# Retention stage of a fused two-block layer: values centred per token, output products with tokens on partitions, row norm per token block, and a new order of the first gate product

## What is computed

```python
u = rms_norm_2(h, ret_norm_pre[i])
q, k, v, g = jnp.split(u @ ret_w_in[i], ...)
q = rope(...); k = rope(...) * (RET_QK_DIM ** -0.5)
o = retention_chunkwise(q, k, v)          # per head: (scores * decay) @ v
mu = jnp.mean(o, axis=-1, keepdims=True)  # over the 512 value columns of a head
var = jnp.mean(jnp.square(o - mu), axis=-1, keepdims=True)
o = (o - mu) * lax.rsqrt(var + EPS)
o = merge_heads(o) * jax.nn.silu(g)
y = o @ ret_w_out[i]                      # 2048 -> 1024
h = h + rms_norm_2(y, ret_norm_post[i])   # norm over the 1024 columns of a token
kv = rms_norm_2(h, kv_norm) @ w_kv        # read by the stick-breaking layer
```

## Time and profile before

| what | value |
|---|---|
| median of 3 runs | 1977.68 us |
| the three runs | 1977.68, 1975.15, 4728.48 us |
| the profiled execution, own time | 1978.11 us |
| its span in the trace | 1976.3 us |
| granted TensorE clock over the span | 0.995 |
| PE busy | 98% |
| DVE busy | 59% |
| ACT busy | 36% |
| HBM read | 169.50 MB |

### The profile page before, as it was taken

How to read it: one execution, slowest core, us unless ns; L and a number is a source line. 1 busy time by engine, 2 the same in 40 slices (tenths; PEclk the granted TensorE clock), 3 DMA queues, 4 the chain that set the end, 5 groups by cost and what they waited for, 6 DMA issues and landing times.

```text
span 1976.3 us, 24001 instructions
## 1 busy us (share of the span) xinstructions
PE 1932.6 (98%) x9302; PEld 1615.8 (82%) x9302; DVE 1172.1 (59%) x1379; ACT 711.1 (36%) x759; POOL 14.2 (1%) x23
## 2 busy tenths in 40 slices
PE   7999999999999999999999999999998999999998
PEld 5888888788878888888888788888886788888886
DVE  5334355677655574434355749494949765556656
ACT  4323233336352233322233223232323644444445
POOL 0000000000000000000000000000000000000000
PEclk9999999999999999999999999999999999999999
DMA  4222223321112222232223322221212112221222
GB/s 169 96 102 89 93 76 101 133 70 63 61 38 99 104 86 107 85 106 85 86 88 102 138 86 86 75 94 65 104 65 85 54 65 86 86 85 68 80 85 65
DMA packets 27448, 173.44 MB, mean 88 GB/s; under 512 B 3200, under 2 KB 3232, under 8 KB 10368
## 3 DMA queue, kind: packets, MB, share of 16 engines
q1 hardware_dynamic: 24912, 165.95, 23.8%
q0 software_dynamic: 1328, 4.61, 0.8%
q10 hardware_dynamic: 1152, 2.10, 0.3%
HBM read 169.50 MB, written 3.15 MB: 87 GB/s over the span
## 4 chain that ended last, share of the span: by engine, by line
PE 91%; DVE 5%; ACT 3%; issue 1%; DMA 0%; DVEq 0%; ACTq 0%
PE acc L1524 27%; PE acc L1525 27%; PE acc L1526 27%; PE att L1525 2%; PE att L1526 2%; PE att L1524 2%; ACT tmp L542 1%; PE att L1935 1%; PE att L1934 1%; ACT tmp L534 1%; DVE w_lo L837 0%; PE att L1964 0%; DMA h<-in_x 0%; PE att L1562 0%; PE att L1980 0%
## 5 line engine op out<-in xcount | busy, mean ns | idle before, releaser
L1524 PE MATMUL acc<-x_hi,w_hi 128*128 128x512 f32 x1400 | 551.4, 394 | 14.8 <-DVE w_lo L837 14.7
L1526 PE MATMUL acc<-x_hi,w_lo 128*128 128x512 f32 x1400 | 546.4, 390 | 0.0
L1525 PE MATMUL acc<-x_lo,w_hi 128*128 128x512 f32 x1400 | 546.3, 390 | 0.0
L837 DVE TENSOR_TENSOR w_lo<-raw,w_hi 128x2048 fp32r<-128x2048 f32 (+1 forms) x166 | 378.5, 2280 | 127.5 <-ACT w_hi L411 123.7
L411 ACT ACTIVATE w_hi<-raw 128x2048 fp32r<-128x2048 f32 (+1 forms) x166 | 315.2, 1899 | 105.7 <-PE acc L1526 101.8
L1524 PEld LDWEIGHTS acc<-x_hi,w_hi 128*128 128x128 f32 x1400 | 263.6, 188 | 72.7 <-DVE w_lo L837 16.1
L1525 PEld LDWEIGHTS acc<-x_lo,w_hi 128*128 128x128 f32 x1400 | 263.5, 188 | 56.3 <-issue 2.4
L1526 PEld LDWEIGHTS acc<-x_hi,w_lo 128*128 128x128 f32 x1400 | 263.4, 188 | 55.5
L1524 PE MATMUL acc<-g_hi,w_hi 128*128 128x512 f32 x352 | 137.2, 390 | 0.0
L1526 PE MATMUL acc<-g_hi,w_lo 128*128 128x512 f32 x352 | 137.1, 389 | 0.0
L1525 PE MATMUL acc<-g_lo,w_hi 128*128 128x512 f32 x352 | 137.1, 389 | 0.0
(11 more groups left out here) (315 smaller groups left out, 2871.9 us busy)
## 6 DMA issues: line engine op xcount, KB each, us to landing
raw<-in_ffn_up SPq DMA_DIRECT2D x44, 1024.0 KB, 4.7
raw<-in_ret_head SPq DMA_DIRECT2D x24, 1024.0 KB, 4.7
raw<-in_ffn_down SPq DMA_DIRECT2D x32, 704.0 KB, 4.0
raw<-in_mix_gate SPq DMA_DIRECT2D x8, 1024.0 KB, 4.7
raw<-in_ret_out SPq DMA_DIRECT2D x8, 1024.0 KB, 4.7
raw<-in_sb_v SPq DMA_DIRECT2D x8, 1024.0 KB, 4.7
raw<-in_sb_kq SPq DMA_DIRECT2D x8, 1024.0 KB, 4.7
raw<-in_sb_g SPq DMA_DIRECT2D x8, 1024.0 KB, 4.7
```

The source lines that it names most:

```text
L837: tt(w_lo[:, slot, 0:cols], raw[:, slot, 0:cols], w_hi[:, slot, 0:cols].bitcast(F32), ALU.subtract).then_inc(w_ready, 1)
L1524: mm(dst, still[0], move[0], start=first, stop=False)
L1525: mm(dst, still[0], move[1], start=False, stop=False)
L1526: return mm(dst, still[1], move[0], start=False, stop=last)
```

## The change

Six things are changed; the arithmetic of the rest stays.

1. Values. ACT reads each bank of values twice: a copy with scale -1/512 whose accumulator gives minus the mean of the token (`neg_mean`), and a second one that adds it as a bias. DVE's low part uses the same number. As the mean over value columns is linear, the head's outputs then have mean zero. The scale of the token (`r_tok`), which the values carried, goes to the scores.
2. The mean of the outputs (L1856), the copies out of `att`, the three additions and the four subtractions go. ACT squares the outputs in `att`, DVE multiplies them there with the gate and frees the bank, and three additions give the sum of squares.
3. The output product takes tokens on partitions: the gated outputs are the stationary side, the weights (laid out anew) the moving one. It has as many passes as before. The norm of the head becomes one number per token (`norm_columns`: four float32 products of 128 columns, issued before the fourth bank), and one DVE instruction per bank scales and adds.
4. In the last head both gate pairs come before `rs` x `rv`, and the output product starts with each gated chunk as it comes.
5. The norm over a token's 1024 columns is taken on ACT by the accumulator of a square, for each block of 128 tokens; ACT scales the first half of the block, DVE the second, and 32 transposes of 128 x 128 float32 on PE (`turn_y`, `turn_y_late`) bring the result back to features on partitions, 16 ahead of the first `kv` chunk and 16 among the chunks. DVE then makes `h` in one instruction from `att`. Of the 36 unread products 6 and 8 are left. The slab of the keys is made in quarters.
6. The first gate product of the mixture comes before the attention branch's products, the second behind them.

```diff
@@ ScalarE, values
+                    nc.scalar.activation(rv_hi[:, k, :], bank, ACT.Copy, scale=-1.0 / TOK,
+                                         accum_out=neg_mean[:, k:k + 1]).then_inc(act_step, 1)
+                    act.wait_ge(act_step, step.next())
+                    nc.scalar.activation(rv_hi[:, k, :], bank, ACT.Identity, bias=neg_mean[:, k:k + 1]).then_inc(hi_ready, 1)
...
@@ ScalarE, last head, second half of the columns
+                    for m in range(TB):
+                        if m == TB - 1:
+                            prep_part(0)
+                        square_rows(1, m)
...
+                        nc.scalar.activation(row_std[:, m:m + 1], half_sq[:, 1, m:m + 1], ACT.Sqrt, scale=1.0 / D,
+                                             bias=half_mean[:, m:m + 1]).then_inc(fn_ready, 1)
+                        act.wait_ge(row_scaled, m + 1)
+                        nc.scalar.activation(y_ret[:, 2 * m, :], y_ret[:, 2 * m, :], ACT.Copy,
+                                             scale=row_scale[:, m:m + 1]).then_inc(z_first, 1)
...
@@ VectorE
+            def gated(c):
+
+                dve.wait_ge(fn_ready, fn.next())
+                dve.wait_ge(sq_ready, squared.next())
+                tt(r_gate[:, c, :], att[:, b.k % BANKS, :], r_gate[:, c, :], ALU.mult).then_inc(att_free, 1)
+                b.next()
...
+                    for m in range(TB):
+                        outputs(1, m, m + 1)
+                        if m == TB - 1:
+                            prep_part(0, keys_part_ready)
+                        scale_rows(m)
+                        if m == 1:
+                            prep()
...
@@ TensorE
-                pair()
-                pe.wait_ge(op_ready, op.next())
-                mm(side_bank(), mean_v[:], t(4), start=True, stop=True).then_inc(att_full, 1)
-                pair()
...
+                def norm_columns():
+
+                    pe.wait_ge(ssq_ready, sq.at())
+                    dst = side_bank()
+                    b.next(RET_SKIP)
+                    for m in range(TB):
+                        ins = mm(dst[:, m:m + P], ssq[:, plain[m]], mean_v[:], start=True, stop=True)
+                    ins.then_inc(att_full, 1 + RET_SKIP)
...
+                    if last and m >= 2:
+                        if m == 2:
+                            turned_y.extend((side_bank(), side_bank(), side_bank(), side_bank()))
+                        turn_y(turned_y, m - 2)
...
+                turn_y(turned_y, TB - 2)
                 keys, query, vals = bank(), bank(), [bank(), bank()]
...
+                spare(6)
+                turn_y(turned_y, TB - 1)
+                spare(8)
...
                 for c in range(DC):
+                    if 1 <= c <= DC - TB:
+                        turn_y_late(c + TB - 1)
...
+                        gate = slab()
+                        project(gate, DC, x)
+                        pe.wait_ge(att_free, b.at(BANKS))
+                        for k in range(2):
+                            project(branch[0], 6 * k, (o_hi, o_lo), 2)
+                        project(gate, 0, x)
```

More of the change, by code:

```diff
@@ L661, in gate, with square_head, split_gated, square_rows @@
                     s.next()
-            def outputs(first, end, last):
-                for c in range(first, end):
-                    val.next()
-                    if last:
-                        act.wait_ge(val_ready, val.at())
-                        square(c, y_ret[:, c, :])
+            def square_head(c):
+                act.wait_ge(att_full, b.next())
+                nc.scalar.activation(r_sq[:, c, :], att[:, (b.k - 1) % BANKS, :], ACT.Square).then_inc(sq_ready, 1)
+            def split_gated(c, first, dst):
+                act.wait_ge(att_free, b.at(first - b.k + c + 1 + BANKS))
+                nc.scalar.activation(dst[:, c, :], r_gate[:, c, :], ACT.Copy).then_inc(hi_ready, 1)
+            def square_rows(half, m):
+                act.wait_ge(acc_free, u.at(m + 1) + BANKS)
+                nc.scalar.activation(t(m), y_ret[:, 2 * m + half, :], ACT.Square,
+                                     accum_out=half_sq[:, half, m:m + 1]).then_inc(act_step, 1)
+                step.next()
             def ret_body(last):
@@ L679, in ret_body @@
                 gate(r_gate[:, 0:2, :])
[L680 to L683 removed]
+                if last:
+                    gate(r_gate[:, 2:4, :])
+                first = b.k
+                if last:
+                    for c in range(RET_VC + 1):
+                        if c < RET_VC:
+                            square_head(c)
+                        if c:
+                            split_gated(c - 1, first, by_chunk(rqk_hi))
+                else:
+                    for c in range(RET_VC):
+                        square_head(c)
+                    gate(r_gate[:, 2:4, :])
                     prep()
                     s.next(2)
[L686 to L688 removed]
+                    for c in range(RET_VC):
+                        split_gated(c, first, rv_hi)
                     prep()
@@ L1829, in ret_values, with turn_y, turn_y_late @@
                         ins.then_inc(seg_done, 1)
+            def turn_y(banks, m):
+                pe.wait_ge(z_first, m + 1)
+                for c in range(TB):
+                    ins = nc.tensor.transpose(banks[c][:, plain[m]], y_ret[:, 2 * m, plain[c]], ident[:])
+                    if m == TB - 1:
+                        ins.then_inc(att_full, 1)
+            def turn_y_late(c):
+                pe.wait_ge(h_ready, 2 * DC + c - TB + 1)
+                dst = att[:, b.k % BANKS, :]
+                b.next()
+                for m in range(TB):
+                    if c == TB:
+                        pe.wait_ge(z_second, m + 1)
+                    ins = nc.tensor.transpose(dst[:, plain[m]], y_ret[:, 2 * m + 1, plain[c - TB]], ident[:])
+                ins.then_inc(att_full, 1)
             def ret_body(last):
@@ L1841, in ret_body @@
                 ret_values(slab(), v_banks, 1)
-                if not last:
+                pair()
+                if last:
                     pair()
@@ L1866, in ret_body @@
-                for j in range(2):
-                    w = slab()
-                    for o in range(4):
-                        project(w, 4 * o, (rv_hi, rv_lo), 4, wait=normed if j + o == 0 else None)
+                    pair()
+                    pair()
+                sq.next()
+                def norm_columns():
+                    pe.wait_ge(ssq_ready, sq.at())
+                    dst = side_bank()
+                    b.next(RET_SKIP)
+                    for m in range(TB):
+                        ins = mm(dst[:, m:m + P], ssq[:, plain[m]], mean_v[:], start=True, stop=True)
+                    ins.then_inc(att_full, 1 + RET_SKIP)
@@ L1871, in _ @@
+                return turned_y
             for o in range(2):
@@ L1977, in sb_start @@
                 op.next(DC)
+                w = slab()
+                dst = att[:, b.k % BANKS, :]
+                b.next()
                 for c in range(DC):
-                    pe.wait_ge(sq_ready, 2 * DC + c + 1)
-                    done = mm(dst, mean_d[:], y_ret[:, c, :], start=c == 0, stop=c == DC - 1)
+                    pe.wait_ge(sq_ready, DC + RET_HEADS * RET_VC + c + 1)
+                    done = mm(dst, mean_d[:], kv_sq[:, c, :], start=c == 0, stop=c == DC - 1)
                 done.then_inc(att_full, 1)
```

317 lines of the change are left out of this document (183 added, 134 removed).

## The result

| | before | after |
|---|---|---|
| median | 1976.60 us (1977.68, 1975.15, 4728.48, 1975.51) | 1958.24 us (1956.73, 1959.76, 1956.21, 1960.56) |
| ratio, 95% interval | 1 | 0.991 [0.989, 0.9929] |
| profiled execution, own time and span | 1978.11, 1976.3 us | 1956.73, 1954.8 us |
| granted clock over the span | 0.995 | 0.999 |

The forecast was 1962.2 us, within 2% of before. The kernel is 0.9% faster, 4 us better than the forecast and inside its range. The run of 4728.48 us, far from all others, counts in the median and not in the ratio. The two profiled executions lie 21.5 us apart in span, and that is more than the change gave. I come to this first, since it decides how every later number is read.

A forecast was written before the change was run, and what follows sets the result against it. PE bounds the kernel, by its work at its pace plus its idle places. Gains of 1.4 + 3.5 + 5.9 + 4.7 = 15.5 us from a median of 1977.68 gave 1962.2 us, 0.8% less; range 1957 to 1969.5.

The forecast's parts named there:

- First gate: PE's 1.48 us wait for `o_lo` at the first gate goes: gain 1.4 us, bounds 0 to 1.5.
- Means: The product with `mean_v` goes in each of four heads, 0.87 us each: gain 3.5 us.
- Last head: Waits around `rs` x `rv` and the output product go, with a clock fall: 5.9 us, besides 0.87 for the mean.
- The three parts named: Last head: wait ahead of `rs` x `rv` 1.61, wait for `rv_lo` 2.57, clock fall 1.7; sum 5.9 us.
- Q: Start of the second output slab in the last head, 1506.87 before; the tail's forecast times count from it.
- Tail: From the second output slab's start to the end of the `kv` chunks: 42.6 becomes 37.9, gain 4.7 us, bounds 1.3 to 8.2.
- The forecast's own case: The granted clock holds at 1.00 in the tail despite waits and transposes; the forecast as a whole has 0.40.
- The rival: Clock falls once or twice in the tail, 1.7 us each: 1963.9 to 1965.6 us; chance 0.27.
- the tail did give something: Answers the rival that the tail gives nothing, through dearer hand-overs or conversions: 1966.9 us, with a fall 1968.6; chance 0.13.
- its waits did appear: Answers the rival that the tail's waits do not appear, first `kv` pass as PE allows: 1958.7 us; chance 0.08.
- no wait stands at the fifth bank of any head: Answers the slower rival: PE waits for the norm in every head, 7.4 us each with a fall: 1991.8 us; chance 0.05.
- the change did all it says: Answers the rival that the first gate's slab is late or a last-head wait stays: 1965 to 1966 us; chance 0.07.

The follow-up runs named there:

- e8_pair_between: Changed kernel with the last head's second gate pair put back behind `rs` x `rv`: 1959.39 us, ratio 0.9919.
- e3_norm_late: Changed kernel with the norm in the first three heads asked for behind the fourth output bank instead of ahead of it: 1963.81 us, ratio 0.9938.
- e9_all_chunks: Changed kernel with the last head's first output slab waiting for all four gated chunks: 1963.92 us, ratio 0.9937.
- e1: Kernel before with only the new order of the first gate put in: 1974.87 us, ratio 0.9993.
- e5: Kernel before without its 36 unread products: 1977.99 us, ratio 1.0016.
- e0: Changed kernel run again, unedited: 1957.15 us, ratio 0.9903.
- e6: Changed kernel with DVE's conversion of the first values' slab moved from behind the second token block to behind the first: 1957.63 us, ratio 0.9912.
- e7: Changed kernel with the edit of e6 and the first quarter of the keys' slab made behind the fourth block's scaling: 1957.42 us, ratio 0.9912.
- e10: Changed kernel with each of the norm's four products of 128 columns issued twice: 1963.40 us, ratio 0.9936.
- e4_no_unread: Changed kernel without its 14 unread products: 1960.62 us, ratio 0.9927.

## Why the prediction was right

**First gate: 1.4 forecast, 1.7 measured** (1.71 in the changed kernel, 1.73 alone). The wait of 1.48 went and the next slab was in time by 0.9 us. The missing 0.3 is in how a bracket counts. It begins at the end of the record in front, and the next pass starts 0.227 us behind the start of a record that is 0.39 long; so a wait costs the pace 0.16 more than its bracket; the first passes behind it start up to 0.31 apart (1482.26 and 1482.57 in e8_pair_between), which is another 0.1. The runs repeat it: a bracket of 0.98 cost 1.25 (e8_pair_between), one of 1.52 cost 1.84 (e3_norm_late).

**Means: 3.5 forecast.** Three heads gave 0.89 each, and doubling the norm's products cost 0.89 and 0.90; the fourth head's share lies in the stretch of the last head and is not measured by itself. The second reading of the values, the squares on ACT and the small reciprocal cost PE nothing, as the forecast had it; no wait stands at a `pair()`.

**Last head: 0.87 + 5.9 forecast, 7.17 measured.** The three parts named were 1.61, 2.57 and the fall of 1.7. All went: no bracket between the values and Q, clock 1.00. The missing 0.4 fits two brackets that each count some 0.2 to 0.3 too little. The chunkwise start was put down as the cause of the second and third, and e9_all_chunks has both back. That the 1.61 went because a pair now stands there is argued from the order; no run took that pair out. One reading was too easy: the first gated chunk was to be ready with three banks of `rs` x `rv` to go, 1.7 us each; its low part ended at 1480.17, 1.7 us ahead of the output product, so one bank was left. And the 1.7 of the fall is a saving only where the fall stands: it does in all three profiles that have this wait of 2.57 us (before, e1, e5).

**Tail: 4.7 forecast, 5.8 measured.** This is the term that was mis-sized. The order of events was right: `w_lo` between block 1 and block 2, a wait ahead of block 2's transposes, two short waits behind it. Each link was a little shorter than I gave it:

| event, from Q | forecast | measured |
|---|---|---|
| block 2 starts on DVE | 10.7 | 10.3 |
| its transposes | 13.6 | 13.25 |
| the wait ahead of them | 1.8 | 1.27 |
| block 3's transposes | 16.3 | 15.6 |
| first `kv` pass | 19.5 | 18.4 |
| end of the `kv` chunks | 37.9 | 36.8 |

The chain of a block was forecast at 3.1 us; for block 1 it is 1501.38 + 0.72 - 1499.32 = 2.8. The five hand-overs, for which I allowed 0.4 us in all, cost 0.04. Between two engines there lie about 0.03 us: DVE's output ends at 1503.99 + 0.74 = 1504.73 and ACT's square starts at 1504.77. And on ACT itself the accumulator's read starts at 1505.31, 0.54 behind the start of a square of 0.63, so these two records overlap by 0.09. The `kv` chunks took the forecast 18.4 (18.43).

**Clock.** The forecast's own case held: 1.00 in the tail, in both windows around the waits, and so in the tails of all eight profiles with these 14 products (after, e0, e3, e6, e7, e8, e9, e10):

```profile
1506.90:1510.30 3.40, 3.06 (x17) 2.38 (x18) 2.29 (x5) 2.07 (x5) 0.00 (x0) 1.00 0.34 142
1510.30:1513.70 3.40, 3.12 (x18) 2.38 (x17) 2.98 (x6) 3.26 (x6) 0.53 (x1) 1.00 0.46 142
```

The rival was the rule of the Trainium skill, "TensorE: Matmul & The Clock Gate", "Part 4: PE-mode transpose", that transposes do not count as activity in the way that products do. By it the prediction had one or two falls in the tail, and none came, with 14 products among and behind the twelve transposes. With the products taken out, the transposes and 4.9 us of idle time were left, and the clock fell (e4_no_unread). The rule would say so too, and so would idle time alone; these runs don't tell the two apart.

**What lay outside the sum.** 4.1 us of the difference between the two profiles come from falls of the clock at 542, at 1580 and at the end, in code that is the same. The prediction's sum was made against one execution that happened to have them. The rest is 1.9 us: 0.3 of gate, 0.4 of last head, 1.1 of tail and 0.1 of heads. Of the 4.0 us between the forecast and the measured median these 1.9 are one part. The other, 2.0, is the starting point: the forecast subtracts from 1977.68, the median of three runs, and fifteen runs of the kernel before have 1975.65. Against the other rivals: the tail did give something, its waits did appear, no wait stands at the fifth bank of any head (a norm asked for a bank later costs 1.84 per head and not 7.4), and the change did all it says.

**What stays open.** Why the same code has the fall at 542, or at 1580, in one execution and not in the next. Why the first gate's 1.7 us show as 0.8 in medians. And whether e6_slab_early beats the changed kernel: 1.23 us by the timeline, nothing by medians 1957.63 and 1957.15, which stem from different groups and whose runs are spread over 1 and 4 us.

## What to carry to other kernels

Where PE bounds, go through its timeline for brackets, and price each as the bracket and 0.2 to 0.3 us more, plus what a lower clock behind it costs; then look at the consumer and let it start with the first piece of its operand (here worth 2.96 us, and 5.8 where the clock fell). Compare two profiles by distances between places that both programs have, not by their spans: here 4 of 21.5 us were not the change's. When a long reduction is replaced by a chain per block, the conversions that stand between the blocks on DVE can set the wait: here moving one by a block gave 1.23 us where the wait was 1.27.

## What the runs showed of the hardware

- The length of the wait in front did not decide alone whether the granted clock fell. Behind 1.52 us it stayed at 1.00 three times (e3_norm_late); behind 2.57 us it fell in all three profiles with that wait; behind the 2.1 to 2.2 us ahead of the place at 1580, in seven of twelve; at 542, with 0.8 to 1.1 us of waiting in front, in six of twelve. 2.96 us brought it to the 1.2 GHz level in the profiled run, for 6.8 us and a price of up to 2.87 above the bracket, where the earlier trace rows showed 3.4 us and 1.7. By the times, two runs of the same kernel had no fall there.
- Waits with brackets of 0.98 and 1.52 cost 0.27 and 0.32 above them, with the clock at 1.00.
- The place at 542 had a fall in the profiles of the kernel before and of the changed kernel's second run, and none in its first. One such fall cost 1.6 us (83.09 and 81.49 us at the place at 1580). Medians of a few runs can so differ by more than an edit of 1 us gives.
- 14 products that nobody reads, set into a serial chain, cost nothing (74.32 us with them and 74.52 without to the first `kv` pass), and the clock was 1.00 with them and 0.50 without. The 36 of the kernel before took 9.97 us in one profile and 11.27 in another (e1_gate_only), and there they held the first `kv` pass back.
- A hand-over from one engine to another took about 0.03 us from the end of a record to the start of the next (ACT behind DVE, DVE behind ACT).
